# A two-layer transformer block on one core: Strassen's scheme over six instead of four of eight row pairs in MLP down, with low parts of summed weights on VectorE

## What is computed

```python
def sq_relu_mlp(h, w1, w2):
    return jnp.square(jax.nn.relu(h @ w1)) @ w2

for i in range(2):
    hn = rmsnorm(h, norm_mix_g[i])
    y = dsa_mixer(hn, ...) if i == 0 else conv_mixer(hn, ...)
    h = h + y
    h = h + sq_relu_mlp(rmsnorm(h, norm_mlp_g[i]), mlp_w1[i], mlp_w2[i])
h = rmsnorm(h, final_g)
h = even_layer(h, ...)
h = odd_layer(h, ...)
```

## Time and profile before

| | |
|---|---|
| median of three runs | 1760.41 us (1759.82 to 1761.57) |
| the profiled execution | 1761.71 us |
| its span in the profile | 1759.6 us |
| granted TensorE clock, mean | 0.998 |
| TensorE busy | 1742.5 us, 99% |
| VectorE busy | 1083.4 us, 62% |
| GpSimd busy | 865.5 us, 49% |
| ScalarE busy | 776.4 us, 44% |

### The profile page before, as it was taken

The page is one execution under the profiler, slowest core; times in us unless marked ns, Lnnn a source line. Parts: engine busy times, 40 slices in busy tenths (PEclk is TensorE's granted clock), DMA queues, the critical chain, the costliest instruction groups (busy, mean ns, idle before and its releaser), DMA issues.

```text
span 1759.6 us, 20741 instructions
## 1 busy us (share of the span) xinstructions
PE 1742.5 (99%) x8017; PEld 1431.0 (81%) x8017; DVE 1083.4 (62%) x1536; ACT 776.4 (44%) x1216; POOL 865.5 (49%) x375
## 2 busy tenths in 40 slices
PE   9999999999999999999999999999999999999998
PEld 7888778888888888888888888877877888888787
DVE  4794543776356599934565357478867950359743
ACT  5524445343234344554343334455545542455542
POOL 4343223576446669834476447544544644334221
PEclk9999999999999999999999999999999999999999
DMA  6232212345334523222345334442333333232111
GB/s 210 74 99 84 61 47 74 105 126 156 95 98 128 154 78 106 71 71 86 97 130 156 96 96 130 146 119 86 97 94 87 93 96 108 71 114 84 55 54 48
DMA packets 113154, 175.11 MB, mean 100 GB/s; under 512 B 12864, under 2 KB 39104, under 8 KB 113056
## 3 DMA queue, kind: packets, MB, share of 16 engines
q1 hardware_dynamic: 113056, 173.79, 32.6%
HBM read 170.09 MB, written 2.10 MB: 98 GB/s over the span
## 4 chain that ended last, share of the span: by engine, by line
PE 92%; DVE 5%; ACT 1%; issue 1%; DMA 1%; POOL 0%; SPq 0%; DVEq 0%; ACTq 0%; POOLq 0%
PE bank L712 27%; PE bank L714 27%; PE bank L713 27%; PE bank L1114 2%; PE bank L1058 1%; PE bank L798 1%; PE bank L898 1%; PE bank L916 1%; PE bank L1273 1%; DVE residual L2175 1%; PE bank L1258 0%; PE bank L906 0%; POOL w_lo L2818 0%; DMA residual<-in_x 0%; DVE gla_r L2657 0%
## 5 line engine op out<-in xcount | busy, mean ns | idle before, releaser
L2818 POOL TENSOR_TENSOR w_lo<-w_raw,w_hi 128x1024 fp32r<-128x1024 f32 (+1 forms) x310 | 785.0, 2543 | 847.2 <-ACT w_hi L1366 847.0
L1366 ACT ACTIVATE w_hi<-w_raw 128x1024 fp32r<-128x1024 f32 (+1 forms) x310 | 323.5, 1055 | 523.8 <-PE bank L714 411.7
L712 PE MATMUL bank<-x_hi,w_hi 128*128 128x512 f32 (+1 forms) x1264 | 502.0, 397 | 0.3 <-DVE x_lo L2603 0.3
L714 PE MATMUL bank<-x_hi,w_lo 128*128 128x512 f32 (+1 forms) x1264 | 492.5, 390 | 0.0
L713 PE MATMUL bank<-x_lo,w_hi 128*128 128x512 f32 (+1 forms) x1264 | 492.0, 389 | 0.0
L712 PEld LDWEIGHTS bank<-x_hi,w_hi 128*128 128x128 f32 (+1 forms) x1264 | 236.8, 187 | 53.8 <-issue 4.6
L713 PEld LDWEIGHTS bank<-x_lo,w_hi 128*128 128x128 f32 (+1 forms) x1264 | 236.8, 187 | 52.5 <-issue 3.8
L714 PEld LDWEIGHTS bank<-x_hi,w_lo 128*128 128x128 f32 (+1 forms) x1264 | 236.7, 187 | 50.6
L712 PE MATMUL bank<-w_hi,f_hi 128*128 128x512 f32 x480 | 187.6, 391 | 0.2 <-DVE residual L2175 0.2
L714 PE MATMUL bank<-w_hi,f_lo 128*128 128x512 f32 x480 | 186.8, 389 | 0.0
L713 PE MATMUL bank<-w_lo,f_hi 128*128 128x512 f32 x480 | 186.8, 389 | 0.0
(11 more groups left out here) (348 smaller groups left out, 2337.5 us busy)
## 6 DMA issues: line engine op xcount, KB each, us to landing
w_raw<-in_mlp_w SPq DMA_DIRECT2D x144, 512.0 KB, 3.8
w_raw<-in_even_w_in SPq DMA_DIRECT2D x48, 512.0 KB, 3.8
w_raw<-in_dsa_w_in SPq DMA_DIRECT2D x28, 512.0 KB, 3.7
w_raw<-in_odd_w_in SPq DMA_DIRECT2D x24, 512.0 KB, 3.7
w_raw<-in_conv_w_pw SPq DMA_DIRECT2D x32, 256.0 KB, 3.1
w_raw<-in_even_w_out SPq DMA_DIRECT2D x16, 512.0 KB, 3.8
w_raw<-in_dsa_w_out SPq DMA_DIRECT2D x8, 512.0 KB, 3.8
w_raw<-in_mlp_w SPq DMA_DIRECT2D x16, 256.0 KB, 3.1
```

Of the source, the lines that this page charges most:

```text
L712: e.matmul(o, sh, mh, start=first, stop=False)
L714: m = e.matmul(o, sl, mh, start=False, stop=last)
L1366: e.activation(hi, src, ACT.Copy).then_inc(*w_hi.up(u))
L2818: e.tensor_tensor(lo, src, hi.bitcast(F32), ALU.subtract).then_inc(*w_lo.up(u))
```

## The change

`PAIRS` goes from 4 to 6. In the first part three pairs stand in a row, then a plain row pair, then three pairs and the last plain one; in the second, three groups and two plain row pairs. A unit more is loaded for each new pair in the first part and for each new group in the second. The low parts of the units that hold sums of weights are made by VectorE (`sum_lo`, with a signal of their own); GpSimd skips them. The room for two more pairs in `f_of_pairs` is that of the four buffers `f_relu`: relu of the four plain blocks now goes to two scratch buffers in turn (`spare` and `rrow`), their squares are written back into their PSUM banks, and rounded and split from there, so that these banks are free only after the split. The order on VectorE around it is new, `second_hi` comes one step later, and the turnings of the new residual are made in the last two plain rows and behind them. In the odd layer three copies of `gv0` stand ahead of `exp_both(1, 1)`, `decay_sums(2, 1)` stands behind the states of head 0, and the first four y blocks are turned in the order 0, 2, 1, 3.

```diff
@@ -67,12 +67,22 @@
-PAIRS = 4
+PAIRS = 6
+PLAIN = 8 - PAIRS
 PAIRED = PAIRS // 2
 HALF_S = S // 2
-DOWN_STEPS = [[("pair", 0), ("plain", 0), ("pair", 1), ("plain", 1), ("pair", 2), ("plain", 2), ("pair", 3), ("plain", 3)],
-              [("group", 0), ("plain", 0), ("group", 1), ("plain", 1), ("plain", 2), ("plain", 3)]]
+DOWN_STEPS = [[("pair", 0), ("pair", 1), ("pair", 2), ("plain", 0), ("pair", 3), ("pair", 4), ("pair", 5), ("plain", 1)],
+              [("group", 0), ("group", 1), ("group", 2), ("plain", 0), ("plain", 1)]]
 STEP_UNITS = {"pair": 2, "plain": 1, "group": 3}
+
+
+def unit_of(n, kind, i, which):
+    at = 0
+    for step in DOWN_STEPS[n]:
+        if step == (kind, i):
+            return at + which
+        at += STEP_UNITS[step[0]]
+
...
@@ -419,8 +429,11 @@
-        def f_raw(c):
-            return FR[:, c, :] if c < 2 * PAIRS else f_relu[c % 4][:, :]
+        def f_relu(c):
+            return FR[:, c, :] if c < 2 * PAIRS else (spare[:, :, :].rearrange("p t n -> p (t n)"), rrow[:, :])[c % 2]
+
+        def f_raw(c, b):
+            return FR[:, c, :] if c < 2 * PAIRS else bank[b][:, :]
...
@@ -490,8 +503,12 @@
         w_hi = signal("w_hi_rounded", every_unit)
-        w_lo = signal("w_lo_split", every_unit)
+        w_lo = signal("w_lo_split", [u for u in every_unit if units[u].added is None])
+        w_lo_sums = signal("w_lo_split_of_sums", [u for u in every_unit if units[u].added is not None])
         used = signal("w_used", every_unit)
+
+        def low_of(u):
+            return (w_lo if units[u].added is None else w_lo_sums).at(u)
...
@@ -1013,12 +1031,14 @@
             c = 2 * PAIRS + 2 * i + kk
-            if half == 1 and row >= 4:
-                turn(row - 4)
-            done_all = i == 8 - PAIRS - 1 and kk == 1
+            for k in ((), (), (0,), (1, 2))[row] if half else ():
+                turn(k)
+            done_all = i == PLAIN - 1 and kk == 1
             two_tiles(Y, c, 0, u, kk, False, done_all)
...
             row += 1
+if half:
+    turn(3)
 for i in range(2):
...
@@ -1033,7 +1053,8 @@
     for j in range(4):
-        free[BANKS[name][j]] = f_squared.at(layer, half, 4 * g + j)
+        made = f_squared if g < PAIRED else f_lo
+        free[BANKS[name][j]] = made.at(layer, half, 4 * g + j)
 down_first(layer, half)
...
@@ -1042,8 +1063,8 @@
 for k in by_features(f"pw1{g}", X, lambda k: x_lo.at(2, k)):
-    if g == 0 and k in (1, 2):
-        for kk in (2 + 2 * k, 3 + 2 * k):
+    if g == 0 and k in (2, 3):
+        for kk in (2 * k, 1 + 2 * k):
             turn_x(2, kk, HIGH[kk % 4])
...
@@ -1309,7 +1330,7 @@
 elif k == 3:
-    for kk in range(4):
+    for kk in Y_ORDER[0:4]:
         turn_y(kk)
...
@@ -1533,11 +1554,16 @@
 for j in range(4):
-    if g > PAIRED:
-        w.wait_ge(*f_lo.at(layer, half, 4 * g - 4 + j))
+    if g >= PAIRED:
+        if j == 0 and spare_free[0] is not None:
+            w.wait_ge(*spare_free[0])
+        elif j >= 2:
+            w.wait_ge(*f_squared.at(layer, half, 4 * g + j - 2))
     elif half:
         w.wait_ge(*f_lo.at(layer, 0, "second", PAIRS - 1))
-    e.activation(f_raw(4 * g + j), bank[BANKS[name][j]][:, :],
+    if g >= PAIRED and j == 2:
+        spare_free[0] = f_squared.at(layer, half, 4 * g + 2)
+    e.activation(f_relu(4 * g + j), bank[BANKS[name][j]][:, :],
                  ACT.Relu).then_inc(*f_kept.up(layer, half, 4 * g + j))
...
@@ -1546,23 +1572,23 @@
             w.wait_ge(*done(f"down{layer}01"))
-        e.activation(FH[:, c, :], f_raw(c), ACT.Copy).then_inc(*f_hi.up(layer, half, c))
-us = list(UNITS[f"down{layer}{half}0"])
+        e.activation(FH[:, c, :], f_raw(c, BANKS[name][j]), ACT.Copy).then_inc(*f_hi.up(layer, half, c))
+us, behind = list(UNITS[f"down{layer}{half}0"]), None
 for kind, i in DOWN_STEPS[0]:
...
         split_to(us.pop(0) + AHEAD)
-    if kind == "plain":
-        second_hi(layer, half, i)
+    if behind is not None:
+        second_hi(layer, half, behind)
+    behind = i if kind == "pair" else None
 us, row = list(UNITS[f"down{layer}{half}1"]), 0
...
         row += 2
-        if half == 1 and row >= 6:
-            for k in (row - 6, row - 5):
-                round_x(n + 1, k, other(BANKS[f"down{layer}11"])[k], done(f"up{layer}13"))
 if half == 1:
+    for k in range(4):
+        round_x(n + 1, k, other(BANKS[f"down{layer}11"])[k], done(f"up{layer}13"))
     add_squares(n + 1, 0)
...
@@ -1907,9 +1934,9 @@
         exps(1, 0)
-    elif k == 5:
-        exp_both(1, 1)
-copy_gv(0, LOW)
+copy_gv(0, LOW, range(T - 1))
+exp_both(1, 1)
+copy_gv(0, LOW, range(T - 1, T))
 exp_left(1, 1)
...
@@ -2157,6 +2184,12 @@
+            def sum_lo(u):
+                src, hi, lo = ring(u)
+                w.wait_ge(*summed.at(u))
+                w.wait_ge(*w_hi.at(u))
+                e.tensor_tensor(lo, src, hi.bitcast(F32), ALU.subtract).then_inc(*w_lo_sums.up(u))
+
             def second_lo(layer, half, p):
...
@@ -2187,18 +2220,23 @@
 first, second = UNITS[f"down{layer}{half}0"], UNITS[f"down{layer}{half}1"]
+pair = [first[unit_of(0, "pair", p, 1)] for p in range(PAIRS)]
+twin = [second[unit_of(1, "group", p // 2, 1 + p % 2)] for p in range(PAIRS)]
 for g in range(4):
...
     if g == 3:
-        first_sum(first[1])
-        first_sum(first[4])
+        first_sum(pair[0])
+        sum_lo(pair[0])
+        first_sum(pair[1])
+        first_sum(pair[2])
     for j in range(4):
...
         w.wait_ge(*f_kept.at(layer, half, c))
-        e.tensor_tensor(f_raw(c), bank[BANKS[f"up{layer}{half}{g}"][j]][:, :], f_raw(c), ALU.mult).then_inc(*f_squared.up(layer, half, c))
+        b = BANKS[f"up{layer}{half}{g}"][j]
+        e.tensor_tensor(f_raw(c, b), bank[b][:, :], f_relu(c), ALU.mult).then_inc(*f_squared.up(layer, half, c))
     for p in range(2 * g, 2 * g + 2) if g < PAIRED else ():
...
@@ -2206,7 +2244,7 @@
 w.wait_ge(*f_hi.at(layer, half, c))
-e.tensor_tensor(FL[:, c, :], f_raw(c), FH[:, c, :].bitcast(F32),
+e.tensor_tensor(FL[:, c, :], f_raw(c, BANKS[f"up{layer}{half}{g}"][j]), FH[:, c, :].bitcast(F32),
                 ALU.subtract).then_inc(*f_lo.up(layer, half, c))
...
@@ -2223,23 +2261,31 @@
         build_toeplitz(e, chunk, j).then_inc(*dve_tapped.up(chunk, j))
-first_sum(first[7])
+sum_lo(pair[1])
+sum_lo(pair[2])
 second_lo(layer, half, 0)
-first_sum(first[10])
+first_sum(pair[3])
+sum_lo(pair[3])
+first_sum(pair[4])
 second_lo(layer, half, 1)
+first_sum(pair[5])
+sum_lo(pair[4])
 second_lo(layer, half, 2)
-second_sum(second[1])
-w.wait_ge(*used.at(first[9]))
+sum_lo(pair[5])
+second_lo(layer, half, 3)
+second_sum(twin[0])
+second_sum(twin[1])
+w.wait_ge(*used.at(first[unit_of(0, "pair", PAIRS - 1, 0)]))
 for i in range(2):
...
     add_product(layer, X2[i], i, 1, -1)
-w.wait_ge(*used.at(first[10]))
+w.wait_ge(*used.at(pair[-1]))
 for i in range(2):
...
     add_product(layer, Y[i], i, 1, 1, down_added, layer, half, "y", i)
-second_sum(second[2])
+sum_lo(twin[0])
 for i in range(2):
...
@@ -2250,12 +2296,20 @@
         add_product(layer, Z[i], i, 0, 1, down_added, layer, half, "z", i)
+sum_lo(twin[1])
+second_sum(twin[2])
+sum_lo(twin[2])
+second_sum(twin[3])
+sum_lo(twin[3])
 for i in range(2):
     add_product(layer, V2[i], 2 + i, 0, 1, down_added, layer, half, "v", i)
-second_lo(layer, half, 3)
-second_sum(second[5])
-second_sum(second[6])
-w.wait_ge(*used.at(second[6]))
+second_lo(layer, half, 4)
+second_lo(layer, half, 5)
+second_sum(twin[4])
+sum_lo(twin[4])
+second_sum(twin[5])
+sum_lo(twin[5])
+w.wait_ge(*used.at(twin[-1]))
 for i in range(2):
...
@@ -2759,9 +2813,9 @@
 decay_sums(2, 0)
-decay_sums(2, 1)
 states(0, 0)
 states(0, 1)
+decay_sums(2, 1)
 decayed(2, 0)
...
@@ -2812,11 +2866,13 @@
 u = split[0]
+split[0] += 1
+if units[u].added is not None:
+    continue
 src, hi, lo = ring(u)
...
 e.tensor_tensor(lo, src, hi.bitcast(F32), ALU.subtract).then_inc(*w_lo.up(u))
-split[0] += 1
...
@@ -2945,7 +3001,7 @@
 if u >= RAW:
-    w.wait_ge(*w_lo.at(u - RAW))
+    w.wait_ge(*low_of(u - RAW))
 if u >= RAW and units[u - RAW].feeds is not None:
```

More of the change, by code:

```diff
@@ L1514, in second_hi @@
             def second_hi(layer, half, p):
-                w.wait_ge(*used.at(UNITS[f"down{layer}{half}0"][3 * p + 1]))
+                w.wait_ge(*used.at(UNITS[f"down{layer}{half}0"][unit_of(0, "pair", p, 1)]))
                 w.wait_ge(*f_lo.at(layer, half, "sums", p // 2))
@@ L1844, in silu_r, with copy_gv @@
                                  scale=stat(5, 2, t)).then_inc(*r_silu.up(n, t))
-            def copy_gv(n, banks):
-                for t, b in enumerate(banks):
+            def copy_gv(n, banks, tiles=range(T)):
+                for t in tiles:
+                    b = banks[t]
                     w.wait_ge(*(tile_mm.at(f"gv{n}", t) if t < T - 1 else done(f"gv{n}")))
@@ L2779, in vector_program @@
                 head_out(1, t)
-            for k in range(4):
+            for k in Y_ORDER[0:4]:
                 split_y(k)
```

23 lines of the change are left out of this document (12 added, 11 removed).

## The result

The changed kernel takes **1791.8 us** (median of 4 runs, 1788.3 to 1798.1), the kernel before 1760.2 beside it: ratio 1.018, 95% interval 1.0165 to 1.0195, or +31.7 us. The forecast was +14.6. The profiled execution has a span of 1790.3 us, 30.7 more than before. One execution of 4001 us, in the run with the signal first, stands apart from all others and is left out of that run's interval.

What follows compares the result with a forecast made beforehand. The prediction took TensorE, busy 99% of the span, as the bound. From 1761.7 us profiled, -10.9 + 29.6 + 0.7 - 4.5 gave 1776.6, or 1775 us as median; its own range was 1765 to 1788, overall 1749 to 1796.

Steps and rivals of the forecast that it cites:

- matmuls: MLP down: two more pairs in each of four halves save 48 matmuls at 0.2267 us, -10.9 us.
- front, with the pieces of the convolution's matrix: After MLP down's first 12 matmuls: 2.3 us bank wait per half; matrix pieces add 3.2 in layer 0, half 0.
- later waits, 4 x 4.3: MLP down behind the front: TensorE waits for residual additions and low parts of summed weights, 4.3 us a half.
- after an MLP: End of an MLP: residual turnings move and VectorE's split precedes the last four additions; +0.7 us, between 0 and 2.
- odd layer: Odd layer: reordered copies, states and y turnings remove waits and slow clock; -4.5 us, at most 5.7, at least 0.
- The lower bound: Front of MLP down: wait of 1.2 us if VectorE is free at E+0.6, E being the last up group's end.
- its walk through VectorE's queue: MLP down, instruction by instruction: VectorE reaches the residual additions at E+42.7; later waits altogether 7.4 us a half.
- VectorE's sums of 1024 columns mostly above 2.5 us: Sign of being right: VectorE's 1024-column sums would mostly last over 2.5 us beside GpSimd's splits.
- The rival of full collision, 1791: MLP down: 9.7 us a half and 4.3 in the first, 43.1 in all, half the odd layer's gain; chance 0.10.
- The lower end, 3.3 us: Later waits per half if VectorE reaches the additions at E+40 because it and GpSimd collide less: 3.3 us.
- the chain of 3.8 us a unit: Last group: sum, ScalarE wait and low part take VectorE 3.8 us per summed unit, TensorE 2.72; 2.9 us late.
- the top of a rival: Full collision's top: waits slow the granted clock, 1.7 us more in each half, giving 1798 us.

Runs made afterwards that it cites:

- the run with the signal first: Changed kernel, GpSimd's low parts of plain MLP-down weights cut to 2 of 1024 columns, a full-length dummy split behind each: 1798.6 us.
- without GpSimd's splits: Changed kernel with GpSimd subtracting only 2 of 1024 columns of each plain MLP-down weight, those low parts left out: 1762.5 us.
- its own run's trace: Kernel before with only the odd layer's new order from the change: 1759.8 us, ratio 0.9992.
- 88 nothing in the other: Kernel before (four pairs) with GpSimd subtracting only 2 of 1024 columns of each MLP-down weight: 1759.8 us, ratio 0.9998.
- the run with the twins on GpSimd: Changed kernel with the low parts of only the second part's weight sums back on GpSimd: 1780.5 us.
- VectorE's low parts out: Changed kernel with VectorE subtracting only 2 of 1024 columns for each summed weight's low part, the rest left out: 1771.9 us.
- all low parts on GpSimd: Changed kernel, six pairs, with the low parts of the weight sums back on GpSimd as in the kernel before: 1801.6 us.

## Why the prediction was wrong

The sign, the places and the kind of the waits were right; the size was half. The sum of the prediction against the trace of the changed kernel (losses by distance of starts, us):

| term | forecast | measured |
|---|---|---|
| matmuls | -10.9 | -10.9 (464 of each where 480 were) |
| front, with the pieces of the convolution's matrix | +12.4 | +12.7 |
| later waits, 4 x 4.3 | +17.2 | +20.6 |
| slow matmuls behind two fronts | 0 | +3.3 |
| other starts in MLP down, most of them right behind a wait | 0 | +2.8 |
| after an MLP | +0.7 | +4.0 |
| odd layer | -4.5 | -2.1 |
| ahead of the first MLP | 0 | +0.3 |
| together | +14.9 | +30.7 |

**The step that failed** is the price of VectorE's lateness in MLP down behind the front: "I take 4.3 us a half", with nothing in the forecast for what comes along with a wait. Measured are 5.2 us a half of waits, 0.8 of slow clock and 0.7 of late starts, 6.7 together; this is 9.5 of the 15.8 us that were missing. The two short terms, the end of an MLP and the odd layer, are 5.7 more.

- *Matmuls at 0.2267 us.* Borne out: without GpSimd's splits MLP down of layer 1, half 0, and the up groups behind it last 167.9 us instead of 168.6. This is 2.7 less for 12 matmuls and 2.0 more that the starts there show as lost.
- *The front, 2.3 us.* Right: 2.40, 2.46 and 2.55 us listed. In layer 0, half 0, 4.66 where 5.5 was forecast. The lower bound was right too: 1.3 once the collision is gone.
- *The later waits, 4.3 us a half.* The prediction had two ends for them, 7.4 us by its walk through VectorE's queue (E+42.7) and 3.3 for an arrival at E+40 that no row gave. In layer 1, half 0, the additions begin at E+43.9, and TensorE loses 1.04, 0.96, 0.2 and 2.5 us where the walk had 1.6, 2.4, 0.5 and 2.9. So the walk came near the moment of arrival, but partly by luck: it had 16.8 us of GpSimd's splits that can't run beside VectorE, where 12.1 us were lost to them, and almost no idle time, where there were 7.0. Its 7.4 us of waits is further from the 5.2 measured than the 4.3 chosen.
- *"VectorE's sums of 1024 columns mostly above 2.5 us"*, named as a sign of being right, did not come. Three of 24 were; the collisions fell mostly on instructions of 512 and 256 columns and on low parts:

```profile
L2176 DVE TENSOR_TENSOR w_raw<-w_raw x24: 1208/1218/3412, 356.7 to 1103.9; 128x1024 f32<-128x1024 f32 x24
```

- *The rival of full collision, 1791*, is the time that was measured, and this is luck. The collisions were not full (1.3 us for each split of 2.4). Its 43.1 us were waits alone, where waits are 33.3 and the rest is the clock, the late starts and the ends of the MLPs.
- *The lower end, 3.3 us*, was wrong in its kind. The prediction put the last group's 2.9 us down to the chain of 3.8 us a unit, collisions or not. With GpSimd's splits gone the chain is unchanged and the wait is 0. So the price of the collisions was not the 4.1 us a half between the two ends but 7.3 (29.3 / 4): all of the later waits, about 1.1 of each front, and part of the slow clock and the late starts.
- *The clock.* It had a part only in the top of a rival. It fell behind two of the four fronts, 1.6 us each (below). So it does not hold that short waits cost nothing beyond themselves: one of the two was 2.46 us long.
- *Starts right behind a wait.* The matmul that follows one starts 0.08 to 0.11 us late, and so do a few others near it; the prediction had nothing for it.
- *The end of an MLP, +0.7.* Behind the first MLP there are new waits for `x_lo` (0.87) and `conv_u` (0.50 and 0.38), 2.7 us in all; behind the second TensorE waits twice for the residual's additions (0.33 each), as it did behind the first before, 1.3 us in all. With GpSimd's splits short both are the same, so the collisions have no part in them.
- *The odd layer, -4.5.* The clock's 1.7 us came. Of the waits, 0.8 went from that for v and 0.2 from those for the states and y; some of this came back in small steps, so that its own run's trace gives 1.9, the changed kernel's 2.1 and the medians 1.4. The term took the edits to remove waits, where for the states they exchanged the last product waited for.

That additions which read a bank do not take part held in every run: in none of the profiles does one of the 120 take over 0.76 us. That the new forms (squares and low parts that read a bank) do not take part is not tested: in the changed kernel none of the 16 squares and 16 low parts lies beside a split.

## What to carry to other kernels

When two engines take turns on a resource, count their time together from the moment at which the queue must arrive, and walk the queue with its idle times: taking away 12.1 us of collisions made the queue only 6.8 us earlier, because idle time took the rest. Then price what comes along with a wait, the clock and the starts behind it, and not the wait alone. An engine without reserve pays for such collisions, and one with reserve for none: 52 splits cost 29 us in one kernel and 88 nothing in the other. Put work that collides beside work that doesn't (here beside additions that read a bank), and when a gap is opened in a queue, ask first whether the next load can fill it.

## What the hardware showed that was not expected

The granted clock fell behind two fronts and not behind two others of the same length. TensorE waited 4.66, 2.40, 2.46 and 2.55 us; stretches behind the third, and behind the fourth (us, then busy times of PE, PEld, DVE, ACT and POOL, granted clock, DMA share, GB/s):

```profile
905.00:908.00 3.00, 1.33 (x5) 1.10 (x6) 3.00 (x6) 3.00 (x7) 0.00 (x0) 0.90 0.00 0
908.00:911.00 3.00, 3.00 (x9) 2.35 (x8) 1.54 (x2) 1.04 (x2) 1.81 (x1) 0.53 0.06 6
...
1083.00:1086.00 3.00, 3.00 (x15) 2.49 (x14) 2.14 (x3) 2.29 (x3) 1.12 (x1) 1.00 0.02 5
```

Nine matmuls in 3 us instead of fifteen: some eight started 0.43 us apart instead of 0.23. The longest wait (4.66) and one of 2.46 us were followed by it. Waits of 2.40 and 2.55 were not, nor was one of 2.54 in the same half of the run with the twins on GpSimd. The other runs widen this: a wait of 1.89 us was followed by it (VectorE's low parts out, 540.6), one of 3.27 was not (all low parts on GpSimd, 960.1). So between 1.9 and 3.3 us the length of a wait alone does not tell, and a front of about 2.5 us is to be priced with either nothing or 1.6 us more.

A dummy split that nobody waits for cost VectorE as much as a needed one: after the run with the signal first, "hidden" work on GpSimd can't be taken as free of cost to VectorE's queue (1188.3 us busy, where the run with short splits alone has 1112.1).
